# Block-inverse levels on 32x32 and 64x64 tiles, z gated in place, and the attention's bias rows on GpSimd's queue

## The reference

```python
a_mat = where(strict, einsum('bhnid,bhnjd->bhnij', kb, k) * decay, 0.0)
ia = a_mat + eye(c)
u = triangular_solve(ia, vb)                      # unit lower triangular
w = triangular_solve(ia, kb * exp(g)[..., None])
...
o = rms_norm(o, norm_w) * silu(z)                 # z: a projection of x
```

```python
pc = masked_softmax(sc + cbias, cdist >= 0)       # cbias[t, c] = rel_bias[bucket(t - cmp_end[c])]
sbias = rel_bias[bucket(t - spos)]
h = gelu(einsum('bclgd,ldh->bcgh', blocks, w1) + b1)   # the compression, once for keys, once for values
```

## Time and profile before

| | |
|---|---|
| Median of 3 runs | 1981.48 us (1977.23 to 1982.14) |
| The profiled execution's own time | 1973.65 us |
| Its span | 1971.9 us |
| Mean granted TensorE clock | 0.978 |
| PE busy | 1886.9 us (96%) |
| DVE, ACT, POOL busy | 54%, 37%, 9% |

### The profile page before, as it was taken

How to read it: one execution, slowest core, us unless ns; L and a number is a source line. 1 busy time by engine, 2 the same in 40 slices (tenths; PEclk the granted TensorE clock), 3 DMA queues, 4 the chain that set the end, 5 groups by cost and what they waited for, 6 DMA issues and landing times.

```text
span 1971.9 us, 24091 instructions
## 1 busy us (share of the span) xinstructions
PE 1886.9 (96%) x9286; PEld 1519.1 (77%) x9286; DVE 1073.8 (54%) x1763; ACT 727.8 (37%) x1293; POOL 180.5 (9%) x81
## 2 busy tenths in 40 slices
PE   7999999999999999999999879899999989999998
PEld 5788898888987788888878668337885768888786
DVE  5548646576553744445543535653515288777434
ACT  4543444634544322121234512663404342222333
POOL 0052333513300000000000000000000000000000
PEclk9999999999999999999999979999999999999998
DMA  5421221211132223333222381002422113232321
GB/s 177 77 54 43 54 65 51 55 56 53 45 109 84 86 86 106 93 98 98 94 92 81 92 145 48 1 1 86 150 80 92 64 64 106 86 105 85 102 75 59
DMA packets 179258, 157.71 MB, mean 80 GB/s; under 512 B 32428, under 2 KB 175337, under 8 KB 179137
## 3 DMA queue, kind: packets, MB, share of 16 engines
q1 hardware_dynamic: 170241, 155.41, 26.6%
q0 software_dynamic: 224, 0.58, 0.5%
q10 hardware_dynamic: 8704, 0.53, 0.3%
HBM read 152.77 MB, written 3.73 MB: 79 GB/s over the span
## 4 chain that ended last, share of the span: by engine, by line
PE 86%; DVE 7%; ACT 3%; SPq 1%; DMA 1%; issue 1%; DVEq 0%; ACTq 0%
PE bank L707 13%; PE bank L709 12%; PE bank L708 12%; PE bank L782 5%; PE bank L784 5%; PE bank L783 5%; PE bank L850 4%; PE bank L851 4%; PE bank L852 4%; PE bank L699 4%; PE bank L960 2%; PE bank L966 2%; PE bank L1208 2%; PE bank L954 1%; PE bank L1191 1%
## 5 line engine op out<-in xcount | busy, mean ns | idle before, releaser
L1334 ACT ACTIVATE w_hi<-ring 128x2048 fp32r<-128x2048 f32 x125 | 239.1, 1913 | 572.9 <-PE bank L709 387.3
L707 PE MATMUL bank<-h_hi,w_hi 128*128 128x512 f32 x1056 | 414.5, 393 | 14.5 <-DVE w_lo L1886 11.4
L708 PE MATMUL bank<-h_lo,w_hi 128*128 128x512 f32 x1056 | 412.4, 391 | 0.0
L709 PE MATMUL bank<-h_hi,w_lo 128*128 128x512 f32 x1056 | 412.4, 390 | 0.0
L1886 DVE TENSOR_TENSOR w_lo<-ring,w_hi 128x2048 fp32r<-128x2048 f32 x102 | 233.5, 2289 | 293.5 <-ACT w_hi L1334 293.5
L707 PEld LDWEIGHTS bank<-h_hi,w_hi 128*128 128x128 f32 x1056 | 199.3, 189 | 59.7 <-DVE w_lo L1886 11.9
L709 PEld LDWEIGHTS bank<-h_hi,w_lo 128*128 128x128 f32 x1056 | 199.1, 189 | 41.9
L708 PEld LDWEIGHTS bank<-h_lo,w_hi 128*128 128x128 f32 x1056 | 199.3, 189 | 41.5 <-issue 0.2
L2570 POOL TENSOR_TENSOR w_lo<-ring,w_hi 128x2048 fp32r<-128x2048 f32 x23 | 105.2, 4575 | 1263.5 <-ACT w_hi L1334 1170.3
L782 PE MATMUL bank<-h_hi,w_hi 128*128 128x512 f32 x432 | 170.5, 395 | 6.3 <-DVE h_lo L1893 5.6
L784 PE MATMUL bank<-h_hi,w_lo 128*128 128x512 f32 x432 | 169.0, 391 | 0.0
(11 more groups left out here) (396 smaller groups left out, 2655.9 us busy)
## 6 DMA issues: line engine op xcount, KB each, us to landing
ring<-in_sc_w_in SPq DMA_DIRECT2D x32, 1024.0 KB, 5.8
ring<-in_gdn_w_in SPq DMA_DIRECT2D x24, 1024.0 KB, 5.3
ring<-in_w_up SPq DMA_DIRECT2D x22, 1024.0 KB, 5.1
ring<-in_gdn_w_out SPq DMA_DIRECT2D x8, 1024.0 KB, 5.2
ring<-in_sc_w_out SPq DMA_DIRECT2D x8, 1024.0 KB, 5.1
ring<-in_w_down SPq DMA_DIRECT2D x8, 1024.0 KB, 5.2
ring<-in_w_in SPq DMA_DIRECT2D x4, 1024.0 KB, 5.8
ring<-in_w_mk SPq DMA_DIRECT2D x4, 1024.0 KB, 5.4
```

The lines of the kernel that those rows point to most:

```text
L707: pe.matmul(o, a_hi(k), b_hi(k), start=(k == 0), stop=False)
L708: pe.matmul(o, a_hi(k), b_lo(k), start=False, stop=False)
L709: mm = pe.matmul(o, a_lo(k), b_hi(k), start=False, stop=(k == KD - 1))
L1334: act.activation(w_hi[:, plan[n]["pair"], :], ring[:, n % 2, :], ACT.Copy).then_inc(w_hi_ready, 1)
```

## The change

Three things are changed together.

1. **Levels.** The products of a level are done on the tiles that are not zero alone: lv 0 on four 32x32 tiles on the diagonal of each 128x128 matrix (16 matmuls for each head and product, 32 rows, 32 columns of weights, 32 moving columns), lv 1 on two 32x32 tiles (8), lv 2 on one 64x64 tile (4). The transposes of lv 2 cover 64x64. Levels 1 and 2 read `A_T` unmasked, with a sign put in by ACT's copy (scale -1), so POOL's eight masks of these levels go, and `level_ready` counts four in each group. ACT's copies and DVE's additions cover the part that is used.
2. **z.** ACT evaluates all four z chunks ahead of the levels, behind its DMAs of L1554. z is written into `gate_out` for groups 0 to 2, where the gating then works in place; the dump of the squares moves to `z_T`; ACT's wait for `gate_ready` goes, its wait for `table_stored` moves ahead of the first z, and `split_hi(6g+7)` moves behind level 2. POOL does its two splits one after the other, behind the four masks.
3. **Bias rows.** The 16 DMAs and the wait for `table_stored` leave SP's queue. POOL's queue issues them after `split_lo` of SC0 and MIX0: eight behind `hid_done` 1, eight behind `hid_done` 2; `split_lo(FF1)` follows.

```diff
--- before.py
+++ after.py
@@ -214,10 +214,11 @@
 decay = turned_Y = other
...
 level_A = [raw[:, 0, :], raw[:, 1, :], raw[:, 2, :], spare[:, 0, :]]
+z_of = lambda g, h: gate_out[:, 4 * g + h, :] if g < GROUPS - 1 else z_T[:, h, :]
 blocks_in, blocks_out = [spare[:, 1, 256 * n:256 * n + 256] for n in range(2)]
...
 block_step = kk[:, 0, 0:64]
-squares_dump = lambda g, h: gate_out[:, 4 * g + h, :] if g < GROUPS - 1 else A_T[:, h, :]
+squares_dump = lambda g, h: z_T[:, h, :] if g < GROUPS - 1 else A_T[:, h, :]
 ln_beta, g_log, G_cum, G_end, e_G, bias0, neg_eG, be_rest, e_end, tmpA, tmpB = [tok[:, n, :] for n in range(11)]
...
 square_sums = lambda g: key_sets[g % 2][0][:, 0:16]
@@ -607,17 +608,7 @@
     for g in range(2):
...
     load(w_in[:, :, 1304:1560], wide(256))
-    sp.wait_ge(table_stored, 32)
-    for a in range(2):
-        for c0 in range(0, NC, 8):
-            n = min(8, NC - c0)
-            sp.dma_start(bias_cmp_T[a][c0:c0 + n, :, :],
-                         bass.AP(tensor=cmp_copies.tensor, offset=480 - 16 * c0 + 4 * a * 8 * CMP_L,
-                                 ap=[[CMP_L - 16, n], [8 * CMP_L, 4], [1, S]])).then_inc(bias_in, 16)
     load_w1(1)
-    for p0 in range(0, P, 16):
-        sp.dma_start(bias_row[p0:p0 + 16], bass.AP(tensor=row_copies.tensor, offset=P - 1 - p0,
-                                                   ap=[[ROW_L - 1, 16], [16 * ROW_L, ATT_H], [1, S]])).then_inc(bias_in, 16)
     for a in range(2):
...
                      w_in[:, :, 256 * f + 128 * a + 64 * c:256 * f + 128 * a + 64 * c + 64]) for f in range(2) for c in range(2)])
@@ -950,21 +941,30 @@
                     pe.wait_ge(y_ready, n0 - 4 + h + 1)
...
                     pe.wait_ge(gate_ready, 4 * g - 3 + h)
-                for t in range(NT):
-                    mm = pe.transpose(psum[4 + h][:, t * P:(t + 1) * P], Y_T[:, h, t * P:(t + 1) * P], ident)
+                w = 64 if lv == 2 else P
+                for t in range(0, S, P):
+                    mm = pe.transpose(psum[4 + h][0:w, t:t + w], Y_T[0:w, h, t:t + w], ident[0:w, 0:w])
                 mm.then_inc(xt_done, 1)
...
                 pe.wait_ge(xt_ready, n0 + h + 1)
-                pe.wait_ge(level_ready, n0 + h + 1)
-                for t in range(NT):
-                    mm = pe.matmul(psum[4 + h][:, t * P:(t + 1) * P], level_A[h][:, t * P:(t + 1) * P],
-                                   turned_Y(g, h)[:, t * P:(t + 1) * P], start=True, stop=True)
+                A, Y, o = level_A[h] if lv == 0 else A_T[:, h, :], turned_Y(g, h), psum[4 + h]
+                if lv == 0:
+                    pe.wait_ge(level_ready, 4 * g + h + 1)
+                for t in range(0, S, P):
+                    for r in range(0, P, 32 << lv):
+                        lo = slice(r, r + (32, 32, 64)[lv])
+                        hi = (lo, slice(r + 32, r + 64), slice(64, P))[lv]
+                        c, d = slice(t + lo.start, t + lo.stop), slice(t + hi.start, t + hi.stop)
+                        mm = pe.matmul(o[hi, c], A[lo, d], Y[lo, c], start=True, stop=True)
                 mm.then_inc(p_done, 1)
...
                 pe.wait_ge(p_ready, n0 + h + 1)
-                for t in range(NT):
-                    mm = pe.matmul(psum[4 + h][:, t * P:(t + 1) * P], level_P(h)[:, t * P:(t + 1) * P],
-                                   Y_T[:, h, t * P:(t + 1) * P], start=True, stop=True)
+                for t in range(0, S, P):
+                    for r in range(0, P, 32 << lv):
+                        lo = slice(r, r + (32, 32, 64)[lv])
+                        hi = (lo, slice(r + 32, r + 64), slice(64, P))[lv]
+                        c, d = slice(t + lo.start, t + lo.stop), slice(t + hi.start, t + hi.stop)
+                        mm = pe.matmul(psum[4 + h][lo, d], level_P(h)[hi, c], Y_T[hi, h, d], start=True, stop=True)
                 mm.then_inc(py_done, 1)
...
         between = iter([(pair, k) for pair in range(2) for k in range(KD)])
@@ -1459,9 +1459,9 @@
                 act.wait_ge(conv_done, 8 * g + n - 2)
...
         else:
-            if g and n == 8:
-                act.wait_ge(gate_ready, 4 * g)
-            act.activation(z_T[:, n - 8, :], psum[c % 4][:, :], ACT.Silu).then_inc(act_out, 1)
+            if g == 0 and n == 8:
+                act.wait_ge(table_stored, 32)
+            act.activation(z_of(g, n - 8), psum[c % 4][:, :], ACT.Silu).then_inc(act_out, 1)
         st["chunk"] += 1
...
             split_hi(6 * g + n // 2 + 2)
@@ -1493,8 +1493,6 @@
     def out_squares(g, v_T, heads):
...
         act.wait_ge(scan_done, HG * NCH * (g + 1))
-        if g == 0:
-            act.wait_ge(table_stored, 32)
         for h in heads:
...
                 ins = act.activation(squares_dump(g, h)[:, t * P:(t + 1) * P], v_T[:, h, t * P:(t + 1) * P], ACT.Square,
@@ -1552,24 +1550,28 @@
             act.wait_ge(blocks_moved, PER_GROUP * g + 160)
...
             act.dma_start(diagonal[1][r, :, r], block_view(inverses_d, b)).then_inc(blocks_moved, 16)
+        for n in range(8, 12):
+            projected(g, n)
+        parts = (lambda v: v, lambda v: v.rearrange("p (t b c) -> p t b c", t=NT, b=2)[:, :, :, 0:32],
+                 lambda v: v.rearrange("p (t c) -> p t c", t=NT)[:, :, 0:64])
         for lv in range(DEEP):
             n0 = 4 * (DEEP * g + lv)
+            upper_rows, lower_rows = (slice(0, 64), slice(64, P)) if lv == 2 else (slice(0, P), slice(0, P))
             for h in range(HG):
...
                     act.wait_ge(p_done, n0 - 4 + h + 1)
-                act.activation(turned_Y(g, h), psum[4 + h][:, :], ACT.Copy).then_inc(xt_ready, 1)
+                act.activation(parts[lv](turned_Y(g, h))[upper_rows], parts[lv](psum[4 + h][:, :])[upper_rows], ACT.Copy)\
+                    .then_inc(xt_ready, 1)
             for h in range(HG):
...
                     act.wait_ge(py_done, n0 - 4 + h + 1)
-                act.activation(level_P(h), psum[4 + h][:, :], ACT.Copy).then_inc(p_ready, 1)
-            if lv < 2:
-                projected(g, 8 + 2 * lv)
-                projected(g, 9 + 2 * lv)
-            if lv == 1:
+                act.activation(parts[lv](level_P(h))[lower_rows], parts[lv](psum[4 + h][:, :])[lower_rows], ACT.Copy,
+                               scale=-1.0 if lv else 1.0).then_inc(p_ready, 1)
+            if lv == 2:
                 split_hi(6 * g + 7)
...
                 for k in range(KD)[3 * lv:3 * lv + 3]:
@@ -2099,7 +2101,7 @@
         for h in range(HG):
...
             dve.scalar_tensor_tensor(out=gate_out[:, 4 * g + h, :], in0=psum[4 + h][:, :], scalar=GNW,
-                                     in1=z_T[:, h, :], op0=ALU.mult, op1=ALU.mult).then_inc(gate_ready, 1)
+                                     in1=z_of(g, h), op0=ALU.mult, op1=ALU.mult).then_inc(gate_ready, 1)
 
...
 
@@ -2161,7 +2163,11 @@
             n0 = 4 * (DEEP * g + lv)
...
                 dve.wait_ge(py_done, n0 + h + 1)
-                dve.tensor_tensor(Y_T[:, h, :], Y_T[:, h, :], psum[4 + h][:, :], ALU.add).then_inc(y_ready, 1)
+                Y, new = [v.rearrange("p (t c) -> p t c", t=NT) for v in (Y_T[:, h, :], psum[4 + h][:, :])]
+                for r, c in ([(slice(0, P), slice(0, P))], [(slice(0, 32), slice(32, 64)), (slice(64, 96), slice(96, P))],
+                             [(slice(0, 64), slice(64, P))])[lv]:
+                    ins = dve.tensor_tensor(Y[r, :, c], Y[r, :, c], new[r, :, c], ALU.add)
+                ins.then_inc(y_ready, 1)
             if not ahead:
...
                     out_low(k, gate_out[:, k, :])
@@ -2578,20 +2584,15 @@
         if g:
...
         pool.memset(Y_T, 0.0).then_inc(y_cleared, 1)
-        for lv in range(DEEP):
-            n0 = 4 * (DEEP * g + lv)
-            for h in range(HG):
-                pool.wait_ge(a_ready, 4 * g + 4)
-                if lv:
-                    pool.wait_ge(p_done, n0 - 4 + h + 1)
-                pool.tensor_tensor(R2(level_A[h]), R2(A_T[:, h, :]),
-                                   masks[:, 7 + lv:8 + lv, :].to_broadcast([P, NT, P]), ALU.mult).then_inc(level_ready, 1)
-            if lv == 0:
-                pool.wait_ge(inverted, g + 1)
-                pool.wait_ge(vb_ready, 4 * g + 4)
-                if g:
-                    pool.wait_ge(ssq_ready, 4 * g)
-                split_lo(6 * g + 6)
+        for h in range(HG):
+            pool.wait_ge(a_ready, 4 * g + 4)
+            pool.tensor_tensor(R2(level_A[h]), R2(A_T[:, h, :]),
+                               masks[:, 7:8, :].to_broadcast([P, NT, P]), ALU.mult).then_inc(level_ready, 1)
+        pool.wait_ge(inverted, g + 1)
+        pool.wait_ge(vb_ready, 4 * g + 4)
+        if g:
+            pool.wait_ge(ssq_ready, 4 * g)
+        split_lo(6 * g + 6)
         split_lo(6 * g + 7)
...
             for n in range(8, 12):
@@ -2599,8 +2600,21 @@
                     pool.wait_ge(conv_done, 8 * g + 16)
...
 
-    for n in (SC0, MIX0, FF1):
-        split_lo(n)
+    split_lo(SC0)
+    split_lo(MIX0)
```

(13 more changed lines are left out.)

## The result

The changed kernel takes 1965.39 us (median of 5 runs, 1960.51 to 1967.94), the kernel before on the same chip 1977.23 (5 runs, 1973.87 to 1982.14): ratio 0.9933, 95% interval 0.991 to 0.9956. It is faster, by some 12 us where 35 were forecast, a third of it.

What follows compares the result with a forecast made beforehand. The prediction took TensorE (PE), busy 96% of the span, as the bound. Levels -25, z +0.6 and rows -10.6 made -35: profiled 1973.65 became 1938.7, plus 7.8 for the median gave 1947 us, range 1923 to 1990.

Steps and rivals of the forecast that it cites:

- The levels (-25): Four level stages: smaller tiles shorten PE's work from 27.35 to 21.1 us a group, -25 us in four.
- the 32 ns: Level products: assumed cost of one pass on a 32x32 tile, 64 ns for a matmul of both passes.
- tiles side by side: Rival in the level stages: tiles overlap and ACT's copies set the pace, -47 us, 1925 us in all; chance 0.13.
- lower bound of 15.6 us a stage: Level stages: time for a stage if tiles run side by side and ACT's copies set the pace, -47 in four.
- the rival of the clock: Level stages: thin tiles drop the clock to 0.50, 1994 us at half a stage; chance 0.13 over f 0.35, 0.07 less.
- my break-even of 0.35: Level stages: share f of a stage at clock 0.50 at which the 35 us saved would be lost.
- z (+0.6 once): Group 0's level stage: Silus and a table load free ACT 1.0 us later, 0.4 of it hidden: +0.6 us.
- The rows (-10.6): Attention's prelude: bias rows off SP's queue let slab MIX0+6 land early, less slab MIX0+7's lateness: -10.6 us.
- sharing half and half: Prelude DMAs: MIX0+7 shares evenly with the rows' 2 MB, its 5.4 us of transfer becoming 10.8.
- as forecast (-13.7): Prelude: gain from MIX0+6 landing early, 11.4 us of PE idle time and 2.3 of clock.
- 3.1 us late: Prelude: slab MIX0+7 lands at 1166.6 against the 1163.5 needed for L1123.
- My worst case: Prelude: MIX0+7 lands behind all bias rows, at 1177, and moving them gives nothing; 1957 us in all, chance 0.10.

Runs made afterwards that it cites:

- e6: e3 with 24 whole 512-column matmuls a group, results unused, one ahead of each head's products in the levels; ratio 0.9951 to the kernel before.
- e2: The changed kernel with the bias rows back on SP's queue, so levels and z alone; ratio 0.9918 to the kernel before.
- e7: e3 with two z chunks behind level 0, two behind level 1, and the split behind level 1; 1951.93 us, ratio 0.9867.
- e1: The kernel before with only the bias rows moved to POOL's queue, levels and z as before; ratio 1.0013, median 1981.55 against 1978.49 us.
- e3: The changed kernel with one more POOL wait: the eight bias_row DMAs are issued once slab MIX0+7 has landed; 1951.13 us, ratio 0.9861.
- e8: The changed kernel with all bias DMAs on SP's queue, the eight of bias_row behind slab MIX0+7's; 1950.35 us, ratio 0.9877.
- e5: e3 with level 0's products on two 64x64 tiles of each block instead of four 32x32; 1937.54 us, ratio 0.9802.
- e9: e5 with four whole 512-column matmuls a group, one ahead of each product of levels 1 and 2 (first head only); ratio 0.9871.
- e10: e5 with eight whole 512-column matmuls a group in levels 1 and 2 (first and third head); ratio 0.9885 to the kernel before.
- e4: The changed kernel with level 0 on whole 128x128 products again, levels 1 and 2 on tiles; ratio 0.9943 to the kernel before.

## Why the prediction was wrong

**The levels (-25): the sum nearly right, by terms that were not, and what lies behind them left out.** Read from the four windows the stages gave 109.6 - 86.4 = 23.2. Three errors cancelled. A 32x32 pass costs 12 to 17 ns, not 32: the 32 ns hold for one tile, and the rival "tiles side by side" was right that tiles overlap. Its lower bound of 15.6 us a stage is close to the 16.4 that e6 gives. Against that stand PE's waits of 9.2 us for instructions, which neither the sum nor a rival had, and the rival of the clock: means of 0.72 to 0.83 in the stages are f = 0.34 to 0.56 at 1.2 GHz, at and over my break-even of 0.35. The kernel still got faster because the break-even was worked out for slow tiles. The step that failed is that the forecast took the clock as 1.00, in the stages and behind them; behind them 7.8 us went. With 1.6 us lost behind the first group's column sums, and 1.3 gained ahead of the fourth stage, where the clock of the kernel before was 0.51 in 472.60 to 476.05 and that of the changed one was not, 23.2 - 7.8 - 1.6 + 1.3 = 15.1, against the 15.0 that the landmarks show at the layer's end. That the sum of -25 came within 2 us of the stages' own 23.2 is luck.

The Trainium skill, TensorEngine Tiling (Array Packing), Gotcha 1 (PSUM Pressure), by which different row tiles cannot access one PSUM bank at once, I had counted against the lower bound. Four row tiles wrote one bank here and their passes started 7 ns apart while one tile takes a pass every 32 ns, so the trace doesn't agree with it as a limit on pace.

**z (+0.6 once).** e2 shows 0.4 us of it in group 0. e7 puts z back and nothing changes. Right as far as can be measured.

**The rows (-10.6): the wrong step is "sharing half and half".** At the end of slab MIX0+6 PE was 13.8 us further ahead, as forecast (-13.7): 11.6 of idle time and 2.3 of clock. The slab MIX0+7 was to land 3.1 us late; it landed as if behind nearly all of the rows, and 13.2 us were given back, with 1.6 more at PE's wait before L1123. My worst case (it lands 23 us after `hid_done` 2, and part 3 is worth nothing) is what happened: it landed after 24.5 us, part 3 cost 1.0 us in the profile, and gained nothing in e1. I had named the place and the mechanism and given it 0.10. The two were asked for within 0.3 us of each other, and 3.1 MB at the 149 GB/s that 1141.2 to 1163.7 moved take 21 us. I had given each half of the bytes. From 1145 to 1157.5 the slab got 615 of the packets and the rows 373, and as a packet of the rows was 16 times as large, the slab got a tenth of the bytes. That the queue of another engine brings no second path was the sentence I drew from the Trainium skill, DMA: Bandwidth & Descriptors (Issuing engines are not separate DMA queues). e3 and e8 agree with it: 0.9861 and 0.9877, whichever engine issues.

**The rest.** 11.8 us by the medians, 7.1 by the profiles. The profiled execution of the kernel before was 3.6 us below its median, that of the changed one 1.2 above. The 7 us behind L1139 are clock in the attention, which falls in other places from one execution to the next (in e1, e2 and e3 too). Twenty executions of the kernel before spread over 12 us (1973.39 to 1985.35), so a difference of a few us between two profiles says nothing here; the landmarks along the trace do.

## What to carry to other kernels

A transfer moved off a crowded queue must also be moved in time: look up what else is released by the same event, and let the one that nobody waits for yet start on the other's landing (14 us from one wait, with either queue). Look at the size of the packets on both sides, too: the side with the small ones gets the smaller part of the bytes. Cutting products down to what is not zero pays until PE runs through its instructions faster than they are brought, and until the clock falls: here 64x64 tiles (32 ns a pass) beat 32x32 tiles (12 ns) by 12 us although they do four times the arithmetic. Price the work behind a thin stage too.

## What was not expected of the hardware

- PE can run out of instructions. Behind 169 to 240 records of 32x32 at 12 ns each it stood for 1.5 to 2.6 us and went on 1.2 to 1.6 us behind the end of a 16 KB transfer of the instruction queue. With 64x64 tiles in level 0 (64 passes a product instead of 128) no such wait is left in e5.
- The granted clock falls from 2.4 to 1.2 GHz during and behind stages of thin tiles, for 10 to 17 us in each group. With a whole product ahead of each head's tiles (e6) it stayed at 2.4 GHz in three groups of four. Four whole products a group (e9) made it no better, eight (e10) did so in one group of four. The waits for instructions aren't what lets it fall: e4 and e5 have none in their stages, and 44.3 us at 0.50.
- Two DMA queues of unequal packets don't share the bytes evenly: 615 packets of 256 bytes went beside 373 of 4096.
- A whole 512-column product between 32x32 tiles costs 0.41 us from start to start, against 0.23 among its like.
